# fp32-accurate column sums in two fp32r passes, one projection unit moved into the block inverse, and weight splits placed anew, in a two-layer hybrid decoder step

## The chip, the cores and the metric

The kernel runs on one core of one Trainium2 chip. The metric is the device time of one execution in microseconds (us). Before the change it is 3319.75 us, the median of 3 runs (3316.57 to 3322.81).

## What is computed

One inference step over 1056 tokens (a prompt of 1024 and 8 sample sequences of 4 tokens) through two decoder layers with width 1024, all in fp32:

```
layer 0: RMSNorm -> one input projection, whose columns feed
           A: dilated sliding-window softmax attention (3 groups of 4 heads, with caches for the samples)
           B: RWKV-7 time mixing, 12 heads of 64 (token shift, decay, delta-rule state, group norm)
         -> [A | B] -> output projection -> residual; RMSNorm -> squared-ReLU MLP (4096) -> residual
layer 1: RMSNorm -> HGRN2, 8 heads of 128 x 128 (forget gate, chunks of 64, output gate)
         -> output projection -> residual; RMSNorm -> squared-ReLU MLP -> residual; final RMSNorm
```

Besides the outputs of the last norm, the window rows of A, the shift rows and the states of B and HGRN2 are returned. In RWKV three sums over the 64 channels of a head and each token matter here: `ss`, the squared length of a key; `bo`, the bonus term r·k·r_k; and `mean` and `var` of the group norm.

## The kernel before, in words

**Tiling.** Activations lie feature-major: 128 partitions, 8 rows (KC) of features, 1056 tokens, worked in NT = 3 chunks of TC = 352 columns. Nearly all matmuls are fp32r, and fp32 accuracy comes from a split: each operand is kept as a high part (rounded to fp32r) and a low part (the rest), and a product is hi·hi + hi·lo + lo·hi. `Kernel.product` (L247) so issues 8 x 3 = 24 matmuls for a chunk of one output tile, called a unit here. `project(i, n, c)` in RWKV is the unit of pair i, tile n and chunk c, and `range(KC // 2)` makes half of one.

**Weights.** SP loads one weight tile of 512 KB at a time into a single buffer `w_raw` (`load_weight`, L209), once POOL has split the one before. POOL makes the high part (L232) and then the low part (L234) in `split_weight` (L223), into one of a few slots; PE waits for POOL's count of splits (`weight_ready`). The order of splits is that of the program, and each waits until PE has read the tile that was last in its slot. In HGRN the first head's four weights are loaded apart, split high by ACT and low by POOL (L4163).

**Stages.** Norm and start (0 to 60 us; `FirstNorm`: squares on ACT, sums over rows on DVE L335, normed rows on DVE L345 and their low parts on DVE L353), attention A (to 465 us), RWKV (465 to 1212 us), output projection 0, MLP 0 (1220 to 1954 us), HGRN (1965 to 2520 us), output projection 1, MLP 1, final norm. The order of the work of each engine is written out by hand; engines meet at named steps (`plan.at(...)`).

**RWKV.** `MixB` runs 6 pairs of heads, one loop turn each, plus a tail. In loop i PE works on pair i and, in between, makes the 9 projection units of pair i+1. The first part of a loop, here called the prelude, has the decay and gate projections (L2608, L2630), units of the next pair, and the sums over channels: `mean` and `var` of the pair before, `ss` and `bo` of this one, each 3 fp32 matmuls against `half_ones` (L2597). A matmul with fp32 operands is two instructions. In the prelude DVE has one long chain: token shifts (L3457 to L3463), the scan of the decays (L3319), and L3324 to L3362, with `rk` at L3359, `bT` at L3360 and `rT` at L3361. ACT does the exponentials, the norms and the evacuations of the units (L2529 to L2535). Then, twice, for blocks G = 0 and G = 1, come the transposes (`pe_turn`, L2725), scores (masked by DVE L3500), an inverse of 128 x 128 triangles by doubling, levels 2, 4, 8, 16 and 32 (`pe_T` L2809, `pe_YX` L2826 and L2829, evacuated by ACT and by DVE's predicated copies L3509), and `pe_solve` (L2850 to L2854). The sample tokens' small matmuls and DVE operations (L3562 to L3568, b_UV) stand in between. Output projection 0 (`EarlyProject`) reads RWKV's result back from DRAM as rows; POOL splits a row in L4398 and L4400, six of them in loop 4, and PE uses them from loop 5 on in place of the next pair's units. PSUM banks in RWKV: two for the units in turn, six for all else in turn (`Turns`; `B.emptied` waits for the last user).

**MLP.** Seven products over half tiles instead of eight, with combined weights (L1064, L1102); ACT evacuates the products (ff_b, L1196) in `keep_both` and stores the squares in `square_out` (L1206).

**HGRN.** Head h has four weight tiles (n = 0 to 3) in four slots, `slot(h, n) = (3, 2, 1, 0)[n]` in each head. The tail of head 7 is woven with output projection 1 (`SplitProject`), whose weights go to slots 0, 1, 2. DVE L4091 makes c_ks, which PE's L3849 reads.

## Time and profile before

| | |
|---|---|
| median of 3 runs | 3319.75 us |
| the profiled execution's own time | 3316.99 us |
| its span (first to last instruction) | 3315.2 us |
| mean granted TensorE clock | 0.983 |
| PE busy / weight load | 96% / 91% |
| DVE, ACT, POOL busy | 66%, 35%, 33% |
| DMA, mean | 97 GB/s |

The page's idle times are those of one engine before an instruction, with what ended them. PE's matmuls overlap in their records, so their starts tell more than their durations. Line numbers are those of the kernel before.

### The profile page before, as it was taken

The page shows a single profiled execution, that of the slowest core. Times are in us where ns is not written, and L with a number is a line of the kernel's source. Part 1 is how long each engine was busy: PE and PEld are TensorE (multiplying, and loading weights), DVE is VectorE, ACT ScalarE, POOL GpSimd, SP SyncE. Part 2 cuts the span into 40 slices and gives each one's busy share as a digit, 9 for nine tenths or more (in the row PEclk, how much of TensorE's full clock was granted, in tenths as well). Part 3 has the DMA queues.
Part 4 walks back from the last instruction along what each step waited for, and adds up shares of the span by engine and source line. Part 5 has one row for each costly group of instructions (what it writes and reads, how often), then busy time and mean ns, then how long its engine had stood idle before and what let it go on. Part 6 is the DMA issues. An engine that isn't in the chain of part 4 may idle for free. (4 is left out here: it accounts for less than half of the span.)

```text
span 3315.2 us, 74986 instructions
## 1 busy us (share of the span) xinstructions
PE 3178.5 (96%) x31728; PEld 3007.5 (91%) x31728; DVE 2171.6 (66%) x3016; ACT 1171.5 (35%) x2377; POOL 1089.3 (33%) x630
## 2 busy tenths in 40 slices
PE   7999889999999989999999999999998999999998
PEld 6999768888888879999999999999997999999998
DVE  5112774665666658666788884566546976668888
ACT  3344222332332434444433352221212444443334
POOL 3322110110114013444455533222202354445543
PEclk9999889999999999999999999999998999999999
DMA  5113540100101112444544411111113144455442
GB/s 167 65 59 103 184 134 9 33 30 9 37 30 53 59 35 74 147 142 141 199 143 143 143 59 58 60 66 60 59 53 117 49 146 143 143 192 169 143 143 92
DMA packets 151200, 322.71 MB, mean 97 GB/s; under 512 B 16904, under 2 KB 50356, under 8 KB 150744
## 3 DMA queue, kind: packets, MB, share of 16 engines
q1 hardware_dynamic: 106480, 242.53, 22.4%
q10 hardware_dynamic: 44392, 75.42, 6.7%
q8 instruction: 253, 4.15, 0.5%
q14 instruction: 75, 0.61, 0.1%
HBM read 227.12 MB, written 93.12 MB: 97 GB/s over the span
## 5 line engine op out<-in xcount | busy, mean ns | idle before, releaser
L247 PE MATMUL psum<-act_hi,w_hi 128*128 128x352 f32 x2088 | 704.7, 338 | 25.1 <-issue 7.3
L247 PE MATMUL psum<-act_hi,w_lo 128*128 128x352 f32 x2088 | 677.6, 325 | 0.0
L247 PE MATMUL psum<-act_lo,w_hi 128*128 128x352 f32 x2088 | 676.6, 324 | 0.0
L232 POOL TENSOR_TENSOR w_hi<-w_raw,derived 128x1024 fp32r<-128x1024 f32 x83 | 163.1, 1965 | 1421.8 <-PE psum L247 1342.9
L247 PEld LDWEIGHTS psum<-act_hi,w_hi 128*128 128x128 f32 x2088 | 397.4, 190 | 54.0 <-issue 23.1
L247 PEld LDWEIGHTS psum<-act_lo,w_hi 128*128 128x128 f32 x2088 | 398.6, 191 | 2.5 <-issue 0.2
L247 PEld LDWEIGHTS psum<-act_hi,w_lo 128*128 128x128 f32 x2088 | 397.8, 190 | 0.0
L1064 PE MATMUL psum<-ff_near,ff_w_hi 128*128 128x264 f32 x2048 | 379.5, 286 | 4.3 <-issue 1.5
L1064 PEld LDWEIGHTS psum<-ff_near,ff_w_hi 128*128 128x128 f32 x2048 | 317.5, 188 | 10.2 <-issue 9.6
L1064 PE MATMUL psum<-ff_far,ff_w_hi 128*128 128x264 f32 x1536 | 286.2, 287 | 8.9 <-ACT ff_b L1196 6.7
L1064 PE MATMUL psum<-ff_near,ff_w_lo 128*128 128x264 f32 x1024 | 291.1, 284 | 0.0
L1064 PEld LDWEIGHTS psum<-ff_far,ff_w_hi 128*128 128x128 f32 x1536 | 240.1, 190 | 10.3 <-issue 9.2
L1102 PE MATMUL psum<-ff_du_odd_lo,ff_dw_odd_hi 128*128 128x264 f32 x832 | 237.6, 286 | 0.0
L1102 PE MATMUL psum<-ff_du_odd_hi,ff_dw_odd_lo 128*128 128x264 f32 x832 | 237.4, 285 | 0.0
L1102 PE MATMUL psum<-ff_du_odd_hi,ff_dw_odd_hi 128*128 128x264 f32 x832 | 236.6, 284 | 0.0
L1471 DVE TENSOR_TENSOR x<-x,psum 128x528 f32<-128x528 f32 x272 | 183.0, 696 | 81.4 <-PE psum L1102 80.8
L1102 PE MATMUL psum<-ff_du_even_hi,ff_dw_even_lo 128*128 128x264 f32 x768 | 219.3, 286 | 0.0
L1064 PE MATMUL psum<-ff_far,ff_w_lo 128*128 128x264 f32 x768 | 219.1, 285 | 0.0
L1102 PE MATMUL psum<-ff_du_even_lo,ff_dw_even_hi 128*128 128x264 f32 x768 | 218.6, 285 | 0.0
L1102 PE MATMUL psum<-ff_du_even_hi,ff_dw_even_hi 128*128 128x264 f32 x768 | 217.9, 284 | 0.7 <-DVE ff_du_even_lo L1456 0.6
L234 POOL TENSOR_TENSOR w_lo<-w_raw,w_hi 128x1024 fp32r<-128x1024 f32 x83 | 214.6, 2586 | 6.5
L943 POOL TENSOR_TENSOR ff_w_lo<-ff_raw,ff_w_hi 128x512 fp32r<-128x512 f32 x94 | 149.5, 1605 | 153.8 <-ACT ff_w_hi L931 103.2
(565 smaller groups left out, 7370.7 us busy)
## 6 DMA issues: line engine op xcount, KB each, us to landing
ff_du_raw<-u SPq DMA_DIRECT2D x224, 264.0 KB, 2.8
w_raw<-weights SPq DMA_DIRECT2D x84, 512.0 KB, 3.3
u<-ff_stage SPq DMA_DIRECT2D x128, 264.0 KB, 2.3
ff_raw<-mlp SPq DMA_DIRECT2D x64, 512.0 KB, 3.9
u<-ff_side SPq DMA_DIRECT2D x96, 264.0 KB, 3.7
s_cache<-cache_a ACTq DMA_DIRECT2D x32, 512.0 KB, 7.1
ff_dt<-mlp SPq DMA_DIRECT2D x64, 256.0 KB, 4.5
ff_dt<-mlp SPq DMA_DIRECT2D x32, 512.0 KB, 7.2
```

The costliest lines, as they stand in the source:

```text
L232: pool.tensor_tensor(hi, raw, self.zeros, ALU.add).then_inc(s.sem, s.step())
L234: pool.tensor_tensor(lo, raw, hi.bitcast(F32), ALU.subtract).then_inc(s.sem, s.step())
L247: last = pe.matmul(out, w[:, k, :], h[:, k, cols], start=(start and k == ks[0] and m == 0), stop=(stop and k == ks[-1] and m == 2))
L943: engine.tensor_tensor(lo, self.weight(w, p), hi.bitcast(F32), ALU.subtract).then_inc(s.sem, s.step(label))
L1064: last = pe.matmul(out, weight[:, k], h[:, tp], start=(p in self.FRESH and k == 0 and t == 0), stop=(k == 3 and t == 2), skip_group_check= ...
L1102: last = pe.matmul(out, w[:, d], u[:, tp], start=(fresh and q == 0 and m == 0), stop=(q == self.WIDTH - 1 and m == 2), skip_group_check=True)
L1471: dve.tensor_tensor(dst, dst, src, op).then_inc(s.sem, s.step(f"dve.{n}.{label}{step}.{d}"))
```

## The change

It has seven parts. (1) Start: weights 1 and 2 are split by ACT (high) and DVE (low) in place of POOL, and the loads of the masks move on ACT's queue to behind `act_third`. (2) MLP: at w == 1 ACT evacuates (`keep_both`) ahead of `square_out` 11. (3) HGRN's first four weights get their low parts from DVE. (4) HGRN's slots rotate from head to head, and the early groups of output projection 1 move. (5) In RWKV POOL's splits of weights 0 and 1 of pairs 2 to 5, and of output projection 0, wait for quiet points of the loop two pairs before. (6) `var` (pairs 0 to 4), `ss` and `bo` are two fp32r passes, over a high part (ACT copy) and a low part (DVE subtract); `mean` and the last `var` stay fp32. Unit (i+1, 0, 2) and its evacuation go ahead of `var` and `ss`. (7) Unit (i+1, 2, 1) moves from behind `bo` into the first inverse, half before `pe_T` 32 and half before `pe_solve`, for i = 0 to 4. Memory is laid out anew for the added tiles.

```
--- before.py
+++ after.py
@@ -162,6 +162,7 @@
         self.half_ones = self.at("half_ones", [P, P], F32, o); o += 512
+        self.half_ones_r = self.at("half_ones_r", [P, P], F32R, o); o += 512
         self.masks = self.at("masks", [P, MASKS, P], U8, o); o += MASKS * P
@@ -232,6 +233,20 @@
         pool.tensor_tensor(lo, raw, hi.bitcast(F32), ALU.subtract).then_inc(s.sem, s.step())
+
+    def act_split(self, act, n):
+
+        s = self.plan.steps["act"]
+        act.wait_ge(self.sem("w_loaded"), (n + 1) * 16)
+        act.activation(self.slots[n][0].rearrange("p k c -> p (k c)"), self.w_raw[:, :], ACT.Copy)\
+            .then_inc(s.sem, s.step(f"act.weight{n}"))
+
+    def dve_split(self, dve, n):
+
+        s = self.plan.steps["dve"]
+        hi, lo = (w.rearrange("p k c -> p (k c)") for w in self.slots[n])
+        dve.wait_ge(*self.plan.at(f"act.weight{n}"))
+        dve.tensor_tensor(lo, self.w_raw[:, :], hi.bitcast(F32), ALU.subtract).then_inc(s.sem, s.step(f"dve.weight{n}"))
@@ -433,10 +448,13 @@
             self.act_square(act, t + 4)
+            if t == 5:
+                self.K.act_split(act, 1)
             self.act_square(act, t)
+        self.K.act_split(act, 2)
         self.act_root(act, 1)
@@ -470,10 +488,12 @@
         self.dve_part(dve, 0, 8)
+        self.K.dve_split(dve, 1)
         for t in range(8, 16):
     def dve_rest(self, dve):
+        self.K.dve_split(dve, 2)
         self.dve_part(dve, 8, 16)
@@ -1267,11 +1287,18 @@
                 self.weight_high(act, w + 1, p)
-            self.square_out(act, w, "11")
-            keep_both(w, 1)
-            for p in (6, 7):
-                self.weight_high(act, w + 1, p)
-            keep_both(w, 2)
+            if w == 1:
+                keep_both(w, 1)
+                self.square_out(act, w, "11")
+                keep_both(w, 2)
+                for p in (6, 7):
+                    self.weight_high(act, w + 1, p)
+            else:
+                self.square_out(act, w, "11")
+                keep_both(w, 1)
+                for p in (6, 7):
+                    self.weight_high(act, w + 1, p)
+                keep_both(w, 2)
             self.weight_high(act, w + 1, 5)
@@ -1541,6 +1568,8 @@
                     self.row_sum(dve, g, q)
+        if self.following is not None:
+            self.following.dve_weights(dve)
         for u in range(16):
@@ -1580,6 +1609,8 @@
         dve.wait_ge(K.sem("constants_loaded"), 6 * 16)
+        dve.tensor_tensor(K.half_ones_r[:, :], K.half_ones[:, :], K.derived[:, 1:2].broadcast_to([P, P]), ALU.add)\
+            .then_inc(K.plan.steps["dve"].sem, K.plan.steps["dve"].step())
         dve.tensor_copy(K.masks[:], K.masks_in[:]).then_inc(s.sem, s.step("dve.setup.masks"))
@@ -2077,7 +2108,12 @@
         K = self.K
+        s = K.plan.steps["pool"]
         for w in range(TILES_A):
+            if w in (1, 2):
+                pool.wait_ge(*K.plan.at(f"dve.weight{w}"))
+                pool.sem_inc(s.sem, s.step() + s.step())
+                continue
             if w >= W_SLOTS:
...
...
@@ -2597,6 +2642,15 @@
+        def split_sums(i, name, high, low):
+            for c in range(NT):
+                cols, out = slice(c * TC, (c + 1) * TC), ps[:, B.of(f"{i}.{name}{c}"), 0:TC]
+                pe.wait_ge(*B.emptied(f"{i}.{name}{c}"))
+                pe.wait_ge(*at(f"dve.B.{i}.{name}_low"))
+                pe.matmul(out, K.half_ones_r[:, :], high[:, cols], start=True, stop=False)
+                pe.matmul(out, K.half_ones_r[:, :], low[:, cols], start=False, stop=True)\
+                    .then_inc(s.sem, s.step(f"pe.B.{i}.{name}{c}"))
+
         for i in range(self.PAIRS + 1):
@@ -2615,12 +2669,13 @@
             unit(i + 1, 0, 1)
+            if not live:
+                sums(i - 1, "var", self.rs, f"act.B.{i - 1}.sq{{c}}")
+                break
+            unit(i + 1, 0, 2)
             if i:
-                sums(i - 1, "var", self.rs, f"act.B.{i - 1}.sq" + ("" if live else "{c}"))
-            if not live:
-                break
-            sums(i, "ss", self.e[4], f"act.B.{i}.kk2")
-            unit(i + 1, 0, 2)
+                split_sums(i - 1, "var", self.sum_high[0], self.rs_low)
+            split_sums(i, "ss", self.sum_high[1], self.e4_low)
             unit(i + 1, 1, 0)
@@ -2633,10 +2688,7 @@
             unit(i + 1, 2, 0)
-            sums(i, "bo", raw[1], f"dve.B.{i}.rk")
-            if i + 1 < self.PAIRS:
-                unit(i + 1, 2, 1)
-
+            split_sums(i, "bo", self.sum_high[0], self.raw_low[i % 2])
             self.pe_turn(pe, i, 0)
@@ -2657,9 +2709,13 @@
             self.pe_YX(pe, i, 0, 16)
+            if i + 1 < self.PAIRS:
+                begin(i + 1, 2, 1)
             self.pe_T(pe, i, 0, 32)
             self.pe_YX(pe, i, 0, 32)
+            if i + 1 < self.PAIRS:
+                end(i + 1, 2, 1)
             self.pe_solve(pe, i, 0)
@@ -3073,6 +3129,9 @@
                 act.activation(rs[:], before[2][:, 0:T], ACT.Square).then_inc(s.sem, s.step(f"act.B.{i - 1}.sq"))
+                act.wait_ge(*at(f"act.B.{i - 1}.sq"))
+                act.wait_ge(*at(f"pe.B.{i - 1}.GWa1e1"))
+                act.activation(self.sum_high[0][:, :], rs[:], ACT.Copy).then_inc(s.sem, s.step(f"act.B.{i - 1}.var_high"))
             evacuate(i + 1, 0, 0)
@@ -3080,6 +3139,8 @@
                     .then_inc(s.sem, s.step(f"act.B.{i}.kk2"))
+                act.wait_ge(*at(f"act.B.{i}.kk2"))
+                act.activation(self.sum_high[1][:, :], self.e[4][:], ACT.Copy).then_inc(s.sem, s.step(f"act.B.{i}.ss_high"))
             evacuate(i + 1, 0, 1)
@@ -3088,6 +3149,7 @@
                     .then_inc(s.sem, s.step(f"act.B.{i}.scale"))
+            evacuate(i + 1, 0, 2)
             if i:
@@ -3102,7 +3164,6 @@
                     .then_inc(s.sem, s.step(f"act.B.{i}.norm"))
-            evacuate(i + 1, 0, 2)
             if live:
@@ -3125,9 +3186,12 @@
             evacuate(i + 1, 1, 1)
+            act.wait_ge(*at(f"dve.B.{i}.rk"))
+            act.activation(self.sum_high[0][:, :], raw[1][:, 0:T], ACT.Copy).then_inc(s.sem, s.step(f"act.B.{i}.bo_high"))
             evacuate(i + 1, 1, 2)
             evacuate(i + 1, 2, 0)
-            evacuate(i + 1, 2, 1)
+            if i + 1 == self.PAIRS:
+                evacuate(i + 1, 2, 1)
@@ -3152,6 +3216,8 @@
                 .then_inc(s.sem, s.step(f"act.B.{i}.sGW"))
+            if i + 1 < self.PAIRS:
+                evacuate(i + 1, 2, 1)
             self.act_solve(act, i, 0)
@@ -3309,10 +3375,17 @@
                         .then_inc(s.sem, s.step(f"dve.B.{i - 1}.mean{c}"))
+            def low_part(owner, name, dst, src, high):
+                dve.wait_ge(*at(f"act.B.{owner}.{name}_high"))
+                dve.tensor_tensor(dst[:, :], src, high[:, :].bitcast(F32), ALU.subtract)\
+                    .then_inc(s.sem, s.step(f"dve.B.{owner}.{name}_low"))
+
             if live:
                 self.shifted(dve, i, 1)
+                if i:
+                    low_part(i - 1, "var", self.rs_low, self.rs[:], self.sum_high[0])
                 dve.wait_ge(*at(f"act.B.{i}.w2"))
@@ -3320,6 +3393,7 @@
                 done(dve.tensor_copy(self.mid[:, 0:NB], tiles[:, :, P // 2 - 1]), "mid")
+                low_part(i, "ss", self.e4_low, e4, self.sum_high[1])
                 dve.wait_ge(*at(L + "mid"))
@@ -3358,6 +3432,7 @@
             done(dve.tensor_tensor(r0, r0, e3, ALU.mult), "bT")
+            low_part(i, "bo", self.raw_low[i % 2], r1, self.sum_high[0])
             done(dve.tensor_tensor(r, r, e4, ALU.mult), "rT")
@@ -3575,7 +3650,13 @@
                     pool.wait_ge(*K.plan.at(before[n]))
+                if i >= 2 and n < 2:
+                    pool.wait_ge(*K.plan.at(self.quiet(i - 2, n)))
                 K.split_weight(pool, self.w0 + 3 * i + n, n)
+
+    def quiet(self, i, n):
+
+        return f"dve.B.{i}." + ("YX32_0w0", "S3")[n]
@@ -3756,8 +3837,15 @@
+    ORDERS = ((3, 2, 1, 0), (2, 3, 1, 0), (2, 1, 3, 0), (1, 2, 3, 0), (1, 2, 0, 3), (1, 0, 2, 3), (0, 1, 2, 3), (0, 1, 2, 3))
+
     def slot(self, h, n):
-        return (3, 2, 1, 0)[n]
+
+        return self.ORDERS[h][n]
+
+    def slot_freed(self, h, slot):
+
+        return f"pe.C.{h}.in{self.ORDERS[h].index(slot)}.{NT - 1}"
@@ -3776,6 +3864,14 @@
+    def dve_weights(self, dve):
+
+        s = self.K.plan.steps["dve"]
+        for n in range(4):
+            hi, lo = (flat(t) for t in self.K.slots[self.slot(0, n)])
+            dve.wait_ge(*self.K.plan.at(f"act.C.weight{n}"))
+            dve.tensor_tensor(lo, self.first_raw[n][:, :], hi.bitcast(F32), ALU.subtract).then_inc(s.sem, s.step(f"dve.C.weight{n}"))
+
     def out_rows(self, h, out):
@@ -3797,9 +3893,9 @@
             if h >= self.HEADS:
-                if 3 <= m < 6:
+                if m in (2, 3, 5):
                     for j in range(2):
-                        out.early_group(pe, j, m - 3, j, self.unit_before(h, j))
+                        out.early_group(pe, j, (2, 3, 5).index(m), j, self.unit_before(h, j))
                 elif 6 <= m < 10:
@@ -4158,12 +4254,11 @@
         for n in range(4):
-            hi, lo = (flat(t) for t in K.slots[self.slot(0, n)])
-            pool.wait_ge(*K.plan.at(f"act.C.weight{n}"))
-            pool.tensor_tensor(lo, self.first_raw[n][:, :], hi.bitcast(F32), ALU.subtract).then_inc(s.sem, s.step() + s.step())
+            pool.wait_ge(*K.plan.at(f"dve.C.weight{n}"))
+            pool.sem_inc(s.sem, s.step() + s.step())
         for h in range(1, self.HEADS):
             for n in range(4):
-                pool.wait_ge(*K.plan.at(f"pe.C.{h - 1}.in{n}.{NT - 1}"))
+                pool.wait_ge(*K.plan.at(self.slot_freed(h - 1, self.slot(h, n))))
                 K.split_weight(pool, self.w0 + 4 * h + n, self.slot(h, n))
@@ -4531,11 +4626,11 @@
             rwkv.pool(pool, [f"pe.low.in{n}.{NT - 1}" for n in range(3)])
-            out0.pool(pool, [f"pe.B.5.in{j}.{NT - 1}" for j in range(3)])
+            out0.pool(pool, [rwkv.quiet(rwkv.PAIRS - 2, 0), rwkv.quiet(rwkv.PAIRS - 2, 1), f"pe.B.5.in2.{NT - 1}"])
             K.plan.steps["split"].begin(pool)
             hgrn.pool(pool)
-            out1.pool(pool, [f"pe.C.{KC - 1}.in{n}.{NT - 1}" for n in (3, 2, 1)])
+            out1.pool(pool, [hgrn.slot_freed(KC - 1, slot) for slot in range(3)])
             mlp1.pool(pool)
@@ -4544,10 +4639,10 @@
             norm_mix0.act_first(act)
-            setup.act_masks(act, K)
             norm_mix0.act_second(act)
             norm_mix0.act_third(act)
+            setup.act_masks(act, K)
             attention.bias_spread(act)
```

## Rows read from the trace of the kernel before

**Rows 1.** The page, busy us, share of the span, instructions of each engine.

```profile
PE 3178.5 (96%) x31728; PEld 3007.5 (91%) x31728; DVE 2171.6 (66%) x3016; ACT 1171.5 (35%) x2377; POOL 1089.3 (33%) x630
```

**Rows 2.** PE in pair 1: start us, us, engine, line, operation, tiles, form.

```profile
603.28 1.94 PE L2597 MATMUL psum<-b_rs,half_ones 128*128 128x352 f32 x6
605.05 1.94 PE L2597 MATMUL psum<-b_e,half_ones 128*128 128x352 f32 x6
606.56 0.59 PE L247 MATMUL psum<-act_hi,w_hi 128*128 128x352 f32 x1
606.99 0.33 PE L247 MATMUL psum<-act_lo,w_hi 128*128 128x352 f32 x1
607.15 0.32 PE L247 MATMUL psum<-act_hi,w_lo 128*128 128x352 f32 x1
```

**Rows 3.** PE's waits: what it waited for, us in total, times, longest us.

```profile
PE psum L2850 <- DVE b_YX L3509: 9.5, 8, 1.3
PE psum L1064 <- ACT ff_b L1196: 6.7, 2, 3.4
PE psum L3849 <- DVE c_ks L4091: 6.4, 4, 4.5
PE psum L2809 <- DVE b_YX L3509: 5.5, 6, 0.9
PE psum L247 <- ACT b_raw L2535: 3.0, 1, 3.0
```

**Rows 4.** Timeline of DVE: start, pair 0 (two rows), loop 4.

```profile
21.87 2.66 DVE L353 TENSOR_TENSOR act_lo<-nm_h,act_hi 128x352 fp32r<-128x352 f32 x1
...
482.91 3.02 DVE L3460 SCALAR_TENSOR_TENSOR b_x<-b_x,vec,b_raw 128x1024 f32<-128x1024 f32 x1
...
499.15 1.25 DVE L3360 TENSOR_TENSOR b_raw<-b_raw,b_e 128x1056 f32<-128x1056 f32 x1
...
1049.16 2.79 DVE L3568 TENSOR_TENSOR b_UV<-b_UV,seq_mask 32x512 f32<-32x512 f32 x1
```

**Rows 5.** Timeline of PE in pair 1's first turn and first inverse.

```profile
634.43 0.60 PE L2725 MATMUL psum<-ident,b_e 128*128 128x128 f32 x4
...
656.17 1.15 PE L2809 MATMUL psum<-b_YX,b_L 64*64 64x64 f32 x32 [0.92 <-DVE b_YX L3509]
...
660.65 0.24 PE L2850 MATMUL psum<-b_YX,b_LZ 64*64 64x64 f32 x1 [1.13 <-DVE b_YX L3509]
```

**Rows 6.** Timeline of DVE in pair 1's prelude.

```profile
611.13 2.79 DVE L3341 SCALAR_TENSOR_TENSOR b_raw<-b_raw,vec,b_rs 128x1056 f32<-128x1056 f32 x1
613.96 3.32 DVE L3344 SCALAR_TENSOR_TENSOR b_raw<-b_raw,vec,b_raw 128x1056 f32<-128x1056 f32 x1
...
625.75 2.95 DVE L3360 TENSOR_TENSOR b_raw<-b_raw,b_e 128x1056 f32<-128x1056 f32 x1
628.62 3.41 DVE L3361 TENSOR_TENSOR b_x<-b_x,b_e 128x1056 f32<-128x1056 f32 x1
```

**Rows 7.** Timeline of POOL: pair 1's prelude, and loop 4.

```profile
612.89 3.28 POOL L234 TENSOR_TENSOR w_lo<-w_raw,w_hi 128x1024 fp32r<-128x1024 f32 x1
...
1042.23 1.95 POOL L4398 TENSOR_TENSOR act_hi<-out_raw,derived 128x1056 fp32r<-128x1056 f32 x1 [41.80 <-DMA out_raw<-mix]
```

**Rows 8.** Timeline of PE: start, loop 4, MLP, the MLP's end, HGRN's tail.

```profile
24.59 0.43 PE L247 MATMUL psum<-act_hi,w_hi 128*128 128x352 f32 x1 [3.47 <-DVE act_lo L353]
...
1052.84 0.34 PE L2826 MATMUL psum<-b_T,b_YX 64*64 64x64 f32 x1 [2.08 <-DVE b_UV L3562]
...
1325.53 0.78 PE L1064 MATMUL psum<-ff_far,ff_w_hi 128*128 128x264 f32 x2 [3.36 <-ACT ff_b L1196]
...
1943.94 0.56 PE L1102 MATMUL psum<-ff_du_last_hi,ff_dw_last_hi 128*128 128x264 f32 x1 [2.17 <-DVE ff_du_last_lo L1456]
...
2507.27 0.63 PE L247 MATMUL psum<-act_hi,w_hi 128*128 128x352 f32 x1 [7.35 <-issue]
```

**Rows 9.** Windows of HGRN's tail (us, busy of PE, PEld, DVE, ACT, POOL, PEclk, DMA).

```profile
2500.00:2505.00 5.00, 0.00 (x0) 0.00 (x0) 4.87 (x8) 0.00 (x0) 2.96 (x2) 0.50 1.03 419
```

More of the change, by code:

```diff
@@ L2419, in __init__ @@
         self.e = [take(f"e{n}", [P, T]) for n in range(5)]
+        self.L = take("L", [P, 2, 4, 64])
+        high_at = a
         self.YX = take("YX", [P, 2, 2, 4, 64])
-        self.L, self.T1, self.LZ = (take(n, [P, 2, 4, 64]) for n in ("L", "T1", "LZ"))
+        self.T1, self.LZ = (take(n, [P, 2, 4, 64]) for n in ("T1", "LZ"))
+        self.sYX = take("sYX", [NS, 2, 2, NS])
+        self.sum_high = [K.at(f"b_sum_high{n}", [P, T], F32R, high_at + n * WIDE) for n in range(2)]
+        assert high_at + 2 * WIDE <= a
         self.KA, self.RB, self.RK = (take(n, [P, 2, 4, P]) for n in ("KA", "RB", "RK"))
+        rs_at = a
         self.rs = K.at("b_rs", [P, T], F32, a)
@@ L2428, in __init__ @@
         self.S = take("S", [P, NB + 1, 64])
-        self.sYX = take("sYX", [NS, 2, 2, NS])
         self.sA = take("sA", [NS, 2, P])
@@ L2446, in __init__ @@
         self.reset = take("reset", [P, T], BF16)
+        raw0_at = a
         self.raw = [[take(f"raw0{n}", [P, RAW]) for n in range(3)], raw1]
+        self.rs_low = K.at("b_rs_low", [P, T], F32R, rs_at)
+        self.e4_low = K.at("b_e4_low", [P, T], F32R, e_at + 4 * WIDE)
+        self.raw_low = [K.at(f"b_raw_low{n}", [P, T], F32R, at + 4 * RAW) for n, at in enumerate((raw0_at, X_AT - 3 * 4 * RAW))]
         self.sL, self.sT1 = (take(n, [NS, 2, NS]) for n in ("sL", "sT1"))
```

## The prediction

> **What bounds the kernel now.** First the page's busy shares [rows 1]: PE is busy 3178.5 us, 96% of the span, the next engine 66%. So the end moves only by what PE issues less, by what PE no longer waits for, or by a clock regained. PE's ends are modelled, therefore I read starts: an fp32r matmul of 352 columns starts 0.16 us after the one before it (the last two lines of [rows 2]), so one projection unit (24 matmuls) is 3.8 us. Then the list of PE's waits [rows 3]: no wait is large, but several small ones stand just where the diff edits: b_YX in the RWKV inverses (9.5 + 5.5), ff_b in the MLPs (6.7), c_ks in HGRN (6.4), b_raw L2535 (3.0). Last the timelines around them.
>
> **The sum, part by part.** It is made against the profiled execution's own 3316.99 us; the median of the runs shown is 2.8 us higher, which I add at the end.
>
> **Column sums in two fp32r passes.** The three fp32 matmuls of a group run from 603.28 to 605.05, 1.77 us [rows 2]. After the change a group is six fp32r matmuls, 6 x 0.16 = 0.96. That is 0.81 less, for 5 var, 6 ss and 6 bo groups: **13.8 us**. The first fp32r matmul after fp32 costs 0.27 more than its pitch (606.56 to 606.99 [rows 2]); such turns go after ss and bo and come twice in the inverse (next part): nought.
> The Trainium skill (FP8 and Floating Point Precision, TensorE Precision Notes) says that true fp32 takes four passes through the array; by that a group would be 12 x 0.16 = 1.92 and the gain 17 x 0.96 = 16.3 us. The row's 1.77 decides.
> What it adds: 17 ACT copies and 17 DVE subtracts of 1056 columns. DVE gets 1.25 us each (the uncontended L3360 of pair 0 [rows 4]), ACT about as much at 1.1. ACT has room; the DVE part is priced below, since the RWKV prelude is where DVE matters.
>
> **The moved unit.** In each pair PE idles before pe_T 32 and before pe_solve: 0.92 and 1.13 us in pair 1 [rows 5]; with the 0.2 us or so that a modelled end hides, 1.1 and 1.3. The first inverses of the other pairs repeat it, and the two sums for b_YX in [rows 3] are these and their siblings in the second inverses, which stay. A half unit is 12 x 0.16 = 1.9 us, longer than either gap, so it fills both: 3.8 issued, 2.4 of it in idle time, and 3.8 gone from the prelude. Five pairs (0 to 4): **12 us**. Its evacuation goes behind sGW on ACT, just before act_solve; I cost it at nothing, since the next unit in that bank is one of the next prelude. If it delayed GW by its 0.47 us, that would take 2.4 us off over the five.
>
> **The prelude's DVE chain.** From 611.1 to 632.0 DVE runs without a break [rows 6], and the first turn starts at 634.43 [rows 5]. Two POOL splits lie beside it (the second half of the first: 3.28 us [rows 7]), and four operations take 2.79, 3.32, 2.95 and 3.41 us instead of 1.25 to 1.3: 7.4 us. The quiet waits take these splits off the stretch: weight 0 goes behind YX32, weight 1 behind S3, where DVE mostly reads PSUM; the weights are read a loop later. What is queued behind these waits on POOL is only the next weights' splits, and behind them on SP the next weight's load, which has the rest of the loop. Against the gain stand 3 new subtracts, 3.7 us, and one wait: L3344 needs ACT's norm, which without the stretched L3341 comes about 1 us late. So rT (L3361) ends 7.4 - 3.7 - 1.0 = 2.7 us earlier, near 629.3. PE comes earlier by the unit and three sum groups, 3.8 + 2.4 = 6.2: at 628.2. It would wait some 1.1 us, first at the bo sums (rk, ACT's copy, the subtract), then at the turn. With a handoff I take -1.3 us for each of pairs 1 to 5, **-6.5 us**; between 0 and -3 per pair. In loop 0 DVE idles ahead of bo, and nothing is lost.
> The change also puts unit (i+1,0,2) and its evacuation ahead of the norm: the 3.0 us wait for L2535 [rows 3], in which ACT stood behind a contended L3460 of 3.02 us [rows 4], goes, and 0.5 of startup with it: **3.5 us**.
>
> **out0's rows.** In loop 4 POOL splits six of out0's rows from 1042.23 on [rows 7], and beside them L3568 takes 2.79 us [rows 4] and PE waits 2.08 for b_UV [rows 8]. After the change these rows run behind S3, past the sample chain: 2.7 us gained. But they then end some 17 us later, 3 to 5 us before loop 5 first reads them, and POOL meets the next prelude. I take **0**, between +3 and -8.
>
> **Start.** POOL's split of weight 1 stretches L353 to 2.66 us where 0.52 is usual [rows 4]; PE waits 3.47 us at 24.59 [rows 8]. The second split does the same to the sums of squares. On ACT and DVE the splits stand in order with the sums, so none is stretched, but each takes 1.1 and 1.2 us of its engine, and the mask DMAs move on ACT to behind act_third, where three evacuations queue behind them. I take **4 us** (1 to 6).
>
> **MLP.** At w == 1 ff_b is evacuated behind square_out 11, which waits for DVE; PE waits 3.36 us [rows 8]. With keep_both ahead of it the wait goes, in both MLPs (6.7 for the two [rows 3]): **6.5 us** (4 to 7). The later store of the square delays nothing that PE reads soon.
>
> **Into HGRN.** POOL's four lows (L4163) run beside the last unit's lows on DVE, and PE waits 2.17 us at 1943.94 [rows 8] and 0.67 before it. On DVE the four take 4 x 1.2 us ahead of the last adds. **2 us** (0 to 3).
>
> **HGRN's tail.** PE waits 4.5 us for c_ks ([rows 3], longest) and 7.35 us for out1's weight 1 [rows 8]; PEclk falls to 0.50 [rows 9], the level of 1.2 GHz, after stretches in which PE stood. With the rotating orders slots 0 to 2 come free in head 7 in the order in which out1 wants them, so weights 0 and 1 can be split before 2490. What is then late next are early_group's rows, loaded in the same time, and c_ks. **8.5 us** (4 to 12): 7.4 of wait and about 4 of half clock, less 3 for the rows. In heads 1 to 6 each weight comes at most a unit later than before, with 25 us in hand: nothing.
>
> Sum: 13.8 + 12 - 6.5 + 3.5 + 0 + 4 + 6.5 + 2 + 8.5 = 43.8. 3317.0 - 43.8 = 3273.2; with 2.8 for the median 3276.
>
> **The rivals.**
> 1. **The low parts become the prelude's bound.** For: DVE's chain is already without a break, and PE arrives 6.2 us earlier. Against: 7.4 us of contention go. At -3.8 instead of -1.3 in five pairs 12.5 us more: 3288.
> 2. **The rows are late in loop 5.** For: 3 to 5 us of slack, and the prelude's two-input operations would be stretched again, each by 2 us. Against: only their last one or two lie there. 8 us: 3284. The Trainium skill (SBUF — State Buffer, Who interferes with whom) says that a DVE instruction with two SBUF inputs and a GpSimd instruction that reads SBUF exclude each other for the whole instruction. L3360 lost 1.7 us and L3344 2.0 beside splits of 1.9 to 3.28 us a half, part of them only; held to the letter the rule would make this rival 12 us, 3288.
> 3. **More than forecast.** The tail gives its 12, the start its 6, and the preludes wait half as long: 3.5 + 2 + 3.3 = 8.8: 3267.
> 4. **Slower.** One mechanism, in the preludes of pairs 1 to 5: copy, handoff and subtract stand in series on the one chain (3 x (1.1 + 1.25) = 7.1 us, and ACT reaches each copy an evacuation of 0.47 late, 1.4), while the splits still fall into the chain. The moved unit then covers nothing and its 3.8 us come back as a wait: 12.3 us a pair, 61.5 in five, in place of 6.5: 3319.75 - 50.3 + 61.5 = 3331. It ends slower from 10 us a pair on. Against it: ACT idles 1 to 3 us at the places where the copies go, and the quiet points lie in another half of the loop.
> That the start and the HGRN entry do nothing is possible: 3282.
>
> **How the numbers follow.** Forecast 0.48, rival 1 0.17, rival 2 0.10, rival 3 0.10, rival 4 0.04; start and entry without effect 0.06; several losses together that end within 0.2% 0.05. All best ends together are 60 us (3259), all worst 13 (3307). For 8 in 10 I leave out the outer ends: 3262 to 3298. A measurement tells about 0.2% (6.6 us) from no change: faster 0.91, same 0.05, slower 0.04.
>
> **What would show it.** In the profile after: fp32 sums left for mean and the last var alone, the new sums' six starts within 1 us; half units where rows 5 had idle; L3341 to L3361 at 1.3 us; a wait of 1 to 2 us at bo or the turn; no ff_b among the waits; out1's splits before 2490 and PEclk 1.00 in the tail. It is wrong if the bo sums or the turn wait over 3 us per pair, if out0's early groups wait in loop 5, or if RWKV as a whole gives less than 15 us (forecast 22.8).

## The result, and the profile after

The changed kernel takes 3280.94 us, the median of 4 runs (3280.22 to 3288.66), against 3318.16 us before (4 runs, 3314.06 to 3322.81): the ratio is 0.9893, 95% interval 0.9872 to 0.9913, so 37 us less. The forecast was 43.8 us less. The profiled execution has a span of 3279.1 us against 3315.2, 36.1 less.

From the page of the changed kernel, the line that answers to [rows 1], and the granted clock in 40 slices:

```profile
PE 3159.3 (96%) x31728; PEld 2993.9 (91%) x31728; DVE 2153.2 (66%) x3040; ACT 1188.3 (36%) x2396; POOL 1058.7 (32%) x622
...
PEclk9999889999999999999999999999999999999999
```

PE's busy time fell by 19 us; the other 17 of the 36 are idle time that went. The clock line is that of the kernel before but for one slice. The list of PE's waits in the changed kernel, for [rows 3]:

```profile
PE psum L262 <- DMA act_lo<-c_lo: 7.1, 1, 7.1
...
PE psum L413 <- DVE nm_acc L350: 4.4, 1, 4.4
...
PE psum L3945 <- DVE c_ks L4187: 3.9, 3, 2.8
PE psum L2906 <- DVE b_YX L3584: 3.8, 3, 1.3
PE psum L1084 <- ACT ff_a L1216: 3.6, 5, 1.1
...
PE psum L2650 <- DVE b_raw_low L3380: 2.6, 1, 2.6
...
PE psum L1084 <- DVE ff_r L1443: 2.1, 2, 1.7
...
PE psum L2865 <- DVE b_YX L3584: 0.9, 1, 0.9
```

The waits for b_YX fell from 9.5 and 5.5 us to 3.8 and 0.9, those for ff_b and b_raw L2535 are gone. New or grown are a DMA (7.1), nm_acc (4.4; before it was 3.4 in two waits, 2.35 at the start and 1.03 at the entry to HGRN, and the 4.4 all stand at that entry), ff_a (3.6 for 1.3), ff_r and b_raw_low. So several waits were replaced, not removed.

To see where the time went I laid the starts of the same matmuls in both traces side by side. It is one trace of each kernel, so a stage's shift also holds what the granted clock did there in that one execution. The shift (start after minus start before, us) at the stage borders, next to the forecast:

| stage | shift in it | forecast |
|---|---|---|
| start, to 60 us | -5.5 | -4 |
| attention, to RWKV | -0.4 | 0 |
| RWKV, loop 0 | -6.4 | |
| loops 1 to 4 | -21.6 | |
| loop 5 | +5.5 | |
| RWKV together | -22.5 | -22.8 |
| MLP 0 | -1.9 | -3.2 |
| into HGRN | -1.4 | -2 |
| heads and tail of HGRN | -2.9 | -8.5 |
| MLP 1 and the rest | -1.7 | -3.2 |

The new sums in pair 1, answering to [rows 2], and the first turn, answering to 634.43 in [rows 5]:

```profile
594.88 0.32 PE L2650 MATMUL psum<-b_sum_high,half_ones_r 128*128 128x352 f32 x1
595.04 0.32 PE L2651 MATMUL psum<-b_rs_low,half_ones_r 128*128 128x352 f32 x1
...
596.66 0.32 PE L2651 MATMUL psum<-b_e_low,half_ones_r 128*128 128x352 f32 x1
...
614.96 0.35 PE L2650 MATMUL psum<-b_sum_high,half_ones_r 128*128 128x352 f32 x1
...
615.78 0.33 PE L2651 MATMUL psum<-b_raw_low,half_ones_r 128*128 128x352 f32 x1
615.95 0.60 PE L2781 MATMUL psum<-ident,b_e 128*128 128x128 f32 x4
```

Twelve matmuls from 594.88 to 596.82 are two groups, 0.97 us each where 1.77 stood. The bo group starts without a wait, and so does the turn. The chain of DVE that feeds them, for [rows 6]:

```profile
601.13 1.31 DVE L3415 SCALAR_TENSOR_TENSOR b_raw<-b_raw,vec,b_rs 128x1056 f32<-128x1056 f32 x1
602.47 1.32 DVE L3418 SCALAR_TENSOR_TENSOR b_raw<-b_raw,vec,b_raw 128x1056 f32<-128x1056 f32 x1
...
612.26 1.25 DVE L3434 TENSOR_TENSOR b_raw<-b_raw,b_e 128x1056 f32<-128x1056 f32 x1
613.50 1.26 DVE L3380 TENSOR_TENSOR b_raw_low<-b_raw,b_sum_high 128x1056 fp32r<-128x1056 f32 x1
614.67 1.25 DVE L3436 TENSOR_TENSOR b_x<-b_x,b_e 128x1056 f32<-128x1056 f32 x1
```

The four operations that POOL had stretched and the new subtract (L3380) take 1.25 to 1.32 us each. L3418 starts with the end of L3415, so the 1.0 us wait for the norm that I had counted isn't there. The subtract ends at 614.76 and PE reads it at 614.96, so that handoff has no margin. rT (L3436, to 615.92) has one: the turn at 615.95 transposes other tiles, and the first matmuls that wait for rT come 3.4 us later:

```profile
619.35 1.16 PE L2839 MATMUL psum<-b_e,b_e 64*128 64x128 f32 x16
```

The same stretch in pair 5:

```profile
1056.29 2.22 PE L2662 MATMUL psum<-b_low,b_low_w 64*128 64x352 f32 x12
...
1072.31 0.40 PE L2650 MATMUL psum<-b_sum_high,half_ones_r 128*128 128x352 f32 x1 [0.96 <-DVE b_e_low L3380]
...
1093.23 0.40 PE L2650 MATMUL psum<-b_sum_high,half_ones_r 128*128 128x352 f32 x1 [2.58 <-DVE b_raw_low L3380]
...
1094.27 0.60 PE L2781 MATMUL psum<-ident,b_e 128*128 128x128 f32 x4
```

Here PE waits 0.96 and 2.58 us for low parts, and 1.0 us twice more in between. From the pair's first matmul to its turn it is 38.0 us; before it was 1123.64 - 1090.07 = 33.6:

```profile
1090.07 2.22 PE L2608 MATMUL psum<-b_low,b_low_w 64*128 64x352 f32 x12
...
1121.86 1.94 PE L2597 MATMUL psum<-b_raw,half_ones 128*128 128x352 f32 x6
1123.64 0.60 PE L2725 MATMUL psum<-ident,b_e 128*128 128x128 f32 x4
```

### The profile page after: what moved, and what is told of

Read it like the earlier page. It is cut to its first block and busy times, and to the rows that moved or that the text cites. A ratio compares the mean times of both kernels' runs of the same rounds, so it can differ in the third digit from the quotient of the medians.

```text
span 3279.1 us, 75033 instructions
## 1 busy us (share of the span) xinstructions
PE 3159.3 (96%) x31728; PEld 2993.9 (91%) x31728; DVE 2153.2 (66%) x3040; ACT 1188.3 (36%) x2396; POOL 1058.7 (32%) x622
## 5 line engine op out<-in xcount | busy, mean ns | idle before, releaser
L262 PE MATMUL psum<-act_hi,w_hi 128*128 128x352 f32 x2088 | 701.8, 336 | 22.8 <-DMA act_lo<-c_lo 7.1
L235 POOL TENSOR_TENSOR w_lo<-w_raw,w_hi 128x1024 fp32r<-128x1024 f32 x81 | 201.0, 2482 | 6.4
```

What stands on the lines that cost most here:

```text
L235: pool.tensor_tensor(lo, raw, hi.bitcast(F32), ALU.subtract).then_inc(s.sem, s.step())
L262: last = pe.matmul(out, w[:, k, :], h[:, k, cols], start=(start and k == ks[0] and m == 0), stop=(stop and k == ks[-1] and m == 2))
```

## The experiments

Each is the changed kernel with one edit, unless it says otherwise. In the code `...` stands for lines left out. Times of four runs differ by up to 10 us in these kernels, so beside the median I give the shift of the same matmuls against the changed kernel's trace, taken across the stage of the edit alone.

How far each can be trusted: the changed kernel was timed only in its own session. The kernel before, timed again beside the experiments, had medians of 3313.6 to 3316.3 us, not 3318.16, so a difference of medians against 3280.94 can be off by some 4 us. The ratio to the kernel before of the same session lies with its whole interval outside the changed kernel's (0.9893, 0.9872 to 0.9913) in three experiments only: the quiet waits taken away, the quiet waits alone, and the three edits together (0.9853, 0.9836 to 0.9869). The sums, the unit and the MLP's order come close to it (0.9919 to 0.9927, their intervals just overlap). The sizes of the smaller edits rest on one trace each, and the clock disturbs these too. Loop 0 is the same code in the changed kernel and in "The loads of groups 1 and 2 later", and there the granted clock stayed at 1.00 where the changed kernel's fell to half (both shown below, at the unit); the loop was 3.8 us shorter. So a stage's shift of less than about 4 us counts only where the waits in the trace explain it.

### The quiet waits taken away

```
-                if i >= 2 and n < 2:
-                    pool.wait_ge(*K.plan.at(self.quiet(i - 2, n)))
...
-            out0.pool(pool, [rwkv.quiet(rwkv.PAIRS - 2, 0), rwkv.quiet(rwkv.PAIRS - 2, 1), f"pe.B.5.in2.{NT - 1}"])
+            out0.pool(pool, [f"pe.B.5.in{j}.{NT - 1}" for j in range(3)])
```

> The changed kernel without the quiet waits: POOL splits the weights in the preludes again. Theory A (the quiet waits make the room in which the fp32r sums and the moved unit pay): in pairs 1 to 4 four DVE operations are stretched by 7 us in all, and since PE now reaches the bo sums without a margin it waits there or at the turn, 4 to 6 us a pair; with loop 0 (2 to 4) and loop 4's sample chain (3) 20 to 30 us slower than the changed kernel: 3301 to 3311. Rival B (the stretch stays hidden, the splits only move): under 8 us slower, 3281 to 3289.

Measured: 3329.86 us (10 runs), 1.0042 of the kernel before (1.0029 to 1.0054), slower than before. Against the changed kernel RWKV is 47 us longer by the trace: 7 in loop 0, 11, 8 and 8 in pairs 1 to 3, 14 in pair 4. PE's waits, then DVE and POOL in pair 1:

```profile
PE psum L2650 <- DVE b_raw_low L3380: 20.4, 6, 4.8
PE psum L262 <- ACT b_raw L2574: 12.0, 5, 3.2
```

```profile
600.66 1.86 DVE L3402 TENSOR_TENSOR b_scale<-b_e,b_mid 128x8 f32<-128x8 f32 x1
...
603.62 2.36 DVE L3528 COPY b_raw<-shift 128x8 f32<-128x8 f32 x1
...
621.19 2.95 DVE L3434 TENSOR_TENSOR b_raw<-b_raw,b_e 128x1056 f32<-128x1056 f32 x1
624.07 3.40 DVE L3380 TENSOR_TENSOR b_raw_low<-b_raw,b_sum_high 128x1056 fp32r<-128x1056 f32 x1
```

```profile
620.63 2.39 POOL L233 TENSOR_TENSOR w_hi<-w_raw,derived 128x1024 fp32r<-128x1024 f32 x1 [14.68 <-PE psum L262]
623.10 3.24 POOL L235 TENSOR_TENSOR w_lo<-w_raw,w_hi 128x1024 fp32r<-128x1024 f32 x1
```

Both bounds of the expectation were too low. The splits follow PE's reads, PE now reads earlier, and the second split falls just on bT and the new subtract: 2.95 and 3.40 us, with PE waiting behind them. DVE loses 3.8 us by it, no more than it lost before, when the split fell on bT and rT (2.95 and 3.41, [rows 6]). New is that PE has nothing left to do meanwhile.

The two engines took turns, operation by operation. The shortest high and low halves of a split in the kernel before take 1.89 and 2.35 us, the two DVE operations without POOL beside them 1.25 and 1.26. End to end that is 6.75 us, and here the four run from 620.63 to 627.47, 6.84 us. The high half waits for the operation before bT, bT for the high half, the low half for bT, and the subtract for the low half. The recorded 5.6 us of the split thus hold 1.4 us of POOL's own waiting. The rule of the Trainium skill that stood in rival 2 (SBUF — State Buffer, Who interferes with whom), by which the two exclude each other for a whole instruction, agrees with these times.

ACT is held too: in its program the evacuations stand behind the norm and the norm waits for DVE, and PE waits 12.0 us for b_raw.

### The quiet waits alone, on the kernel before

```
+                if i >= 2 and n < 2:
+                    pool.wait_ge(*K.plan.at(self.quiet(i - 2, n)))
```

(and the two labels for out0)

> The kernel before with the quiet waits alone. Theory A (before, PE had its unit (2, 1) as cover and did not wait for the stretched chain except at loop 0, loop 4): 4 to 8 us faster than before: 3311 to 3315. Rival B (the splits cost PE their 7 us in every pair): 25 us faster or more, 3293 and below.

Measured: 3310.23 us (10 runs), 0.9989 of before (0.9976 to 1.0002), 3.8 us less, which the interval does not tell from nothing. By the trace 4.3 us come in loop 0, 1.3 at out0's rows in loop 4, and the preludes of loops 1 to 4 together gain 0.8. Theory A holds. The same edit is worth 4 us alone, and 49 by the medians or 47 by the trace under the other parts.

### The sums in fp32 again

In effect (the kernel has it as a condition on the pair, which no pair meets here):

```
-                split_sums(i - 1, "var", self.sum_high[0], self.rs_low)
-            split_sums(i, "ss", self.sum_high[1], self.e4_low)
+                sums(i - 1, "var", self.rs, f"act.B.{i - 1}.sq")
+            sums(i, "ss", self.e[4], f"act.B.{i}.kk2")
...
-            split_sums(i, "bo", self.sum_high[0], self.raw_low[i % 2])
+            sums(i, "bo", raw[1], f"dve.B.{i}.rk")
```

(without the three copies and the three subtracts)

> The changed kernel with var, ss and bo in fp32 again, no copies and no subtracts, the order of the units as changed. Theory A (each group is worth 0.81 us, and pair 5's waits of 1.0, 1.0, 1.0 and 2.6 us come from the added chain): plus 13.8, minus 5 to 7 for pair 5: 7 to 9 us slower, 3288 to 3290. Rival B (the sums gave their full 13.8, pair 5's waits come from the order of the units alone): 13 to 14 slower, 3294 to 3295. Rival C (DVE's subtracts cost as much as PE gains): within 2 us of 3281.

Measured: 3289.68 us, 8.7 more than the changed kernel; by the trace 13.9 more up to loop 4 and 3.0 less in loop 5, 10.9 over RWKV (10.0 over the whole kernel). Theory A: the sums are worth their time in five pairs and cost in the sixth.

### Loop 5 as before

Var of pair 4, ss and bo of pair 5 in fp32, as above but for those alone, and in loop 5 the unit (with its evacuation) behind ss again:

```
-            unit(i + 1, 0, 2)
+            if i not in (5,):
+                unit(i + 1, 0, 2)
...
+            if i in (5,):
+                unit(i + 1, 0, 2)
             unit(i + 1, 1, 0)
```

> The changed kernel, but loop 5 as before: var of pair 4, ss and bo of pair 5 in fp32, without copies and subtracts, and unit (6, 0, 2) in its old place. Theory A (in pair 5 no POOL split stood in the prelude before, and PE had no unit to give away, so the added DVE and ACT work is paid in full; from the start of the pair to its first turn took 33.6 us before and 38.0 after): 4 us faster than the changed kernel, 3277, first turn 33.6 us behind the pair's start. Rival B (pair 5's loss comes from out0's rows and the load of x beside it, not from the sums): within 1.5 us of 3281, 37 to 38 us to the turn.

Measured: 3278.88 us, 2.1 less than the changed kernel in the medians; 4.4 less across loop 5 by the trace. Pair 5, first matmul, bo, turn:

```profile
1056.57 2.22 PE L2662 MATMUL psum<-b_low,b_low_w 64*128 64x352 f32 x12
...
1088.36 1.94 PE L2642 MATMUL psum<-b_raw,half_ones 128*128 128x352 f32 x6
1090.14 0.60 PE L2784 MATMUL psum<-ident,b_e 128*128 128x128 f32 x4
```

33.6 us again. Theory A, and the row loads beside it are cleared. With the sums alone undone loop 5 gained 3.0 (experiment before this one); the other 1.4 would be the unit's place.

### The unit back in the prelude

```
-                begin(i + 1, 2, 1)
...
-                end(i + 1, 2, 1)
...
+            if i + 1 < self.PAIRS:
+                unit(i + 1, 2, 1)
             self.pe_turn(pe, i, 0)
```

(and its evacuation likewise)

> The changed kernel with unit (i+1, 2, 1) whole behind the bo sums again. Theory A (both gaps of the first inverse are filled): 2.4 us a pair, 12 slower: 3293; in the profile the idle 0.9 and 1.1 us before pe_T 32 and pe_solve are back. Rival B (some of the gain went back as half clock or as a wait in the second inverse, as in pair 0, where 3.8 us more than in the trace of before went at the end of the sample chain): 6 to 9 slower, 3287 to 3290.

Measured: 3290.79 us, 9.9 more, and 10.6 in RWKV by the trace: between the two theories. The gaps are back in pair 1:

```profile
639.06 1.15 PE L2863 MATMUL psum<-b_YX,b_L 64*64 64x64 f32 x32 [0.92 <-DVE b_YX L3579]
...
644.11 0.34 PE L2904 MATMUL psum<-b_YX,b_LZ 64*64 64x64 f32 x1 [1.13 <-DVE b_YX L3579]
```

Loop by loop the difference runs from -2 to +8 us, not 2.4 each. Part of it is the granted clock. In loop 0 of the changed kernel it fell to half in the second inverse; the kernel before and, with the same code in loop 0, the kernel of the later loads kept 1.00 there (the changed kernel first, then these two):

```profile
536.00:540.00 4.00, 3.20 (x117) 3.03 (x117) 3.88 (x7) 0.97 (x3) 0.00 (x0) 0.90 0.02 4
540.00:544.00 4.00, 4.00 (x44) 2.39 (x38) 2.33 (x5) 0.00 (x0) 1.75 (x1) 0.50 0.02 4
```

```profile
552.00:556.00 4.00, 3.12 (x134) 2.95 (x131) 3.88 (x7) 0.97 (x3) 0.00 (x0) 1.00 0.01 4
556.00:560.00 4.00, 4.00 (x80) 3.02 (x76) 2.22 (x5) 0.36 (x1) 0.00 (x0) 1.00 0.02 4
```

```profile
538.00:542.00 4.00, 4.00 (x83) 3.02 (x77) 2.28 (x5) 0.30 (x1) 2.11 (x2) 1.00 0.01 4
```

The columns are the stretch and its length, PE, PEld, DVE, ACT and POOL busy, PEclk, DMA share and GB/s. PE's busy time ahead of it was alike (3.20 and 3.12 of 4 us). The half clock cost 3.8 us there, by the shift against either of the two. Some such stretches stand at one place in most of the traces and are missing in a few, and I can't assign them to an edit.

### The tail of HGRN: orders and groups as before

```
-    ORDERS = ((3, 2, 1, 0), (2, 3, 1, 0), ...
+    ORDERS = ((3, 2, 1, 0),) * 8
...
-                if m in (2, 3, 5):
+                if m in (3, 4, 5):
```

> The changed kernel with the slots in HGRN in one fixed order (3, 2, 1, 0) and the early groups at 3, 4 and 5 again. Theory A (the wait for weight 1 went, but another of 7.2 us, for the rows c_hi and c_lo, took its place, and of 8.5 us only 3.5 came): 3.5 us slower, 3284.5, with the 7.4 us wait behind a weight back. Rival B (the tail gave the forecast 8.5, and something else lost 5): 8 to 9 slower.

Measured: 3282.55 us, 1.6 more in the medians, which tells nothing (the ratio to the kernel before is 0.9886, 0.9859 to 0.9913); 3.5 more across the tail. The wait behind a weight is back at 7.27 us, and c_ks's longest is 4.48. Theory A, by the trace. In the changed kernel the tail has these two waits:

```profile
2469.44 0.66 PE L262 MATMUL psum<-act_hi,w_hi 128*128 128x352 f32 x1 [7.10 <-DMA act_lo<-c_lo]
...
2481.11 1.16 PE L3945 MATMUL psum<-c_qp,c_ks 128*64 128x64 f32 x20 [2.77 <-DVE c_ks L4187]
```

```profile
2464.00:2466.00 2.00, 0.00 (x0) 0.00 (x0) 2.00 (x3) 0.91 (x1) 0.00 (x0) 0.57 1.03 414
2466.00:2468.00 2.00, 0.00 (x0) 0.00 (x0) 1.97 (x4) 0.17 (x1) 0.00 (x0) 0.50 1.03 416
```

c_ks is waited for 2.77 us where it was 4.48, and in the place of the weight stands the rows' DMA, under way at over 410 GB/s. The clock falls as before.

### The early groups at 3, 4 and 5, with the rotating orders

```
-                if m in (2, 3, 5):
+                if m in (3, 4, 5):
```

> The changed kernel with the rotating orders, but early groups at 3, 4 and 5 as before. Theory A (group 0 waits for a DMA that lands at one fixed time, 9 us after its issue, wherever the group stands; one later place lets PE do a c_qp product inside that wait): 1 to 2 us faster, 3279 to 3280. Rival B (the c_qp product then waits 4.5 us for c_ks ahead of the group, and both waits add): 2 to 4 slower, 3283 to 3285.

Measured: 3277.63 us, 3.3 less in the medians and 4.0 less across the tail.

```profile
2471.65 1.98 PE L3945 MATMUL psum<-c_qp,c_ks 128*64 128x64 f32 x32 [4.00 <-DVE c_ks L4187]
...
2474.83 0.66 PE L262 MATMUL psum<-act_hi,w_hi 128*128 128x352 f32 x1 [0.95 <-DMA act_lo<-c_lo]
...
2485.03 0.43 PE L262 MATMUL psum<-act_hi,w_hi 128*128 128x352 f32 x1 [1.50 <-DMA act_lo<-c_lo]
```

The c_qp product waits 4.00 us for c_ks inside the time in which the DMA is under way, and then 0.95 and 1.50 are left for the rows: 6.5 us of waits for 9.9. Theory A, and more than it gave. The move of the groups to 2, 3 and 5 worked against the rotation: of its 7.5 us it gave 4 back.

### The loads of groups 1 and 2 later

```
-                for g in range(3):
-                    out.load(act, g)
+                out.load(act, 0)
...
+                if h == self.HEADS - 1 and m == 2:
+                    out.load(act, 1)
+                    out.load(act, 2)
```

> The changed kernel, in which ACT issues the loads of row groups 1 and 2 only behind its copy of row 6, some 4 to 6 us later. Theory A (6.3 MB leave together at about 410 GB/s and share it, so group 0's 2.1 MB land only after 9 us; alone they take 5.2): group 0's wait falls from 7.2 to 3 to 4 us, 1 to 3 us faster in all, 3278 to 3280, since groups 1 and 2 still land at 2475 to 2477. Rival B (the queue is served in order, so group 0 gains nothing and the others come later): 1 to 5 us slower.

Measured: 3276.93 us, 4.0 less in the medians, but 0.1 more across the tail: the medians' difference is from elsewhere. The wait for group 0 is 6.93 us where it was 7.10:

```profile
2465.49 0.66 PE L262 MATMUL psum<-act_hi,w_hi 128*128 128x352 f32 x1 [6.93 <-DMA act_lo<-c_lo]
```

Theory A falls. Group 0's second load was issued at 2456.58 and PE went on at 2465.49, 8.9 us; in the changed kernel it was issued at 2460.37 and PE went on at 2469.44, 9.1 us. The loads behind it came 4.7 us later in the one and within 3 us in the other, so they took nothing from group 0: ACT's queue moved its loads in order here. The later issue cost the other groups nothing either.

### The MLP's old order

```
-            if w == 1:
+            if w == 99:
                 keep_both(w, 1)
                 self.square_out(act, w, "11")
```

No w is 99, so every turn takes the other branch, with `square_out` ahead of `keep_both`.

> The changed kernel with the MLP's order of ACT as before (square_out 11 ahead of keep_both at w == 1). Theory A (of 3.4 us a wait for ff_b, 1.0 to 2.1 come back as waits for ff_a and ff_r of the next products, so 2.6 net in the first MLP and 1.5 in the second): 4 us slower, 3285, both waits of 3.4 us back. Rival B (the new waits have nothing to do with the order): 6.5 slower.

Measured: 3286.13 us, 5.2 more; by the trace 2.7 more across the edited products of MLP 0 and 1.4 across those of MLP 1. PE's waits with the old order:

```profile
PE psum L1084 <- ACT ff_b L1216: 6.7, 2, 3.4
...
PE psum L1084 <- ACT ff_a L1216: 1.3, 2, 0.7
```

The wait for ff_b is back, and that for ff_a is 1.3 where the changed kernel had 3.6, with ff_r's 2.1 not on the list. Theory A.

### HGRN's first low parts on POOL, and late on DVE

```
-            self.following.dve_weights(dve)
...
+            pool.tensor_tensor(lo, self.first_raw[n][:, :], hi.bitcast(F32), ALU.subtract).then_inc(s.sem, s.step() + s.step())
```

> The changed kernel with HGRN's first four low parts on POOL again. Theory A (PE's waits for ff_du_last_lo went, but DVE, which now has four more operations, became the bound: a wait of 4.4 us for nm_acc took their place; DVE's own balance is 7 us less stretch against 4.8 of work): 1.5 to 2 us slower, 3283, with the waits of 0.7 and 2.2 us back and nm_acc's near 1. Rival B (no effect, POOL or DVE): 3281.

Measured: 3283.25 us, 2.3 more, 1.1 across the stage. The 2.8 us for ff_du_last_lo are back, and nm_acc is at 1.7 instead of 4.4. The other way:

```
-            self.following.dve_weights(dve)
+            self.following.dve_weights(dve, (0,))
         for u in range(16):
             self.last_add(dve, u)
             self.after.dve_tail(dve, u)
+            if u == 8 and self.following is not None:
+                self.following.dve_weights(dve, (1, 2, 3))
```

> The changed kernel in which only weight 0's low part stands ahead of the last adds; 1, 2 and 3 come behind the ninth of them, where DVE is idle for 3.75 us. Theory A (DVE bounds the norm's sum there): the wait for nm_acc falls from 4.4 to about 1, 3 to 4 us faster, 3277 to 3278. Rival B (PE then waits for the act_lo rows, which come later by as much): within 1 us of 3281.

Measured: 3277.31 us, 3.6 less, and 5.0 less across the stage.

```profile
PE psum L413 <- DVE nm_acc L350: 1.0, 1, 1.0
```

Theory A both times: DVE was the new bound, and 3.4 us of the wait came from work that could stand later. The other 1.6 of the 5.0 is the clock: the changed kernel was granted 0.57 from 1921 to 1925, behind its longer wait, and this one 1.00 from 1920 to 1928. Whether the shorter wait kept the clock up isn't shown.

### Three edits together

Loop 5 as before, groups at 3, 4 and 5, the low parts behind the ninth add.

> The changed kernel with three edits together: loop 5 in fp32 and in the old order, the early groups at 3, 4 and 5, and the low parts of HGRN's weights 1 to 3 behind the ninth last add. Theory A (they stand in different stages and add): 4.4 + 4.0 + 3.5 = 12 us faster than the changed kernel, 3269. Rival B (half clock falls elsewhere and takes part of it): 3272 to 3276.

Measured: 3265.89 us (3263.59 to 3273.12), 0.9853 of before (0.9836 to 0.9869) and 15 less than the changed kernel. By the trace 4.4, 4.0 and 5.0 us in their stages, 13.3 together. It beats both kernels, and here the runs show it too: the ratio's interval lies below that of the changed kernel. The profiled execution as a whole is only 7.7 us shorter than the changed kernel's; it is the slowest of the four (3273.12). Rival B happened in it: the clock fell to half from 1023 to 1029 us and from 1139 to 1145, where the changed kernel's trace has 1.00:

```profile
1023.00:1029.00 6.00, 6.00 (x48) 4.11 (x48) 1.95 (x4) 0.00 (x0) 4.57 (x3) 0.50 0.01 3
```

## Why the prediction was right, and where it was not

- **Right in sign and range.** 3280.94 against 3276, in 3262 to 3298; 37 us of the 44 came. Some single terms were further off than the sum, so part of the agreement is luck. Of the signs that I named, the sums, the filled gaps, the 1.3 us operations and the missing ff_b came; PEclk 1.00 in the tail did not (0.50 from 2464 to 2474), and the wait at bo came in pair 5 alone.
- **Sums, 13.8.** The size of a group is right (0.97 us for 0.96, against the row's 1.77). The sum counted 17 groups; those of loop 5 brought no gain, since the chain there had no slack. What came is 8.7 by the medians, 10.9 across RWKV by the trace.
- **Unit, 12.** 9.9 with it undone. The mechanism holds (both gaps filled), the size was off, and half clock that fell in loop 0 and pair 1 of one trace and not of the other is part of that; how large a part stays open.
- **The prelude's -6.5.** The step that failed. I spread it as -1.3 over pairs 1 to 5. Pairs 1 to 4 show no wait for a low part: the 1.0 us wait for the norm did not come, and the turn, which I had waiting for rT, does not read it (its reader comes 3.4 us later). Pair 5 lost 6.8 alone, the 4.4 us by which its stretch grew and the 2.4 that three shorter groups should have taken off. I had seen that the quiet waits remove contention, and had not asked in which pair there was none: pair 5's L3341 to L3361 ran at 1.3 us before, so the subtracts are bare cost there, and PE, which before started the bo sums 31.8 us after the pair's first matmul, now waits until 36.9 for the last of them. The term came right by two errors that cancel, which is luck.
- **The quiet waits.** I costed the loss of cover at 7.4 us a pair. Taken away it is 47 us in all, 8 to 14 in each of pairs 1 to 4, as the splits are tied to PE's own progress and follow the chain. My rival 4 (12.3 us a pair, slower than before) is what then happens, at 10.2 on average. It needed exactly the condition that I gave it, that the splits still fall into the chain.
- **Loop 0, 3.5; rows, 0.** The waits of loop 0 gave 5.4 (4.1 for L2535, 1.3 at the first ss), and half clock in its second inverse took 3.8 away. Loop 4 gave 3.6 us more than its unit and sums. The rows account for 1.3 of it, which they gave alone; the rest may be the clock, granted 0.52 from 1052 to 1059 in the kernel before and 1.00 in this part of the changed kernel's trace. Rival 2 did not come: nothing waits for a row in loop 5. Its reading of L3360 and L3344, that they lost only part of a split, was wrong: they lost nearly what the split's halves take without DVE beside them, as the first experiment's times show.
- **Start, 4.** 5.5, in the range of 1 to 6. PE's waits of 3.47 and 2.35 us there fell to 0.2 and nothing, two new ones of 0.4 and 1.7 for the splits' count came, and the clock was at half three times between 18 and 39 us before and once after. It was not undone in an experiment, so which of its edits gave it, and how much is the clock, stays open.
- **MLP, 6.5.** 4.1. "The later store delays nothing that PE reads soon" was wrong: the next products wait 2.3 us more for ff_a and 2.1 for ff_r.
- **Into HGRN, 2.** 1.4, but the mechanism was only half seen: PE gained 6.3 us at the last units and gave 4.9 back, 3.4 of them to nm_acc (1.0 before, 4.4 now).
- **Tail, 8.5.** The term most wrong: 3.5. I named the rows as late next and took 3 us for them; it was 7.1, since group 0 was asked for earlier (at 2) and its two loads of 1056 KB come 9 us after their issue. The clock's loss, for which I had 4, stayed for the most part: half clock for 17 us before, for 13.5 after.

## What to carry to other kernels

When work leaves PE's stretch and other work is added to the engine that feeds it, ask for each turn of the loop apart what slack that engine has: the last turn differs. A contention that costs nothing today may be what bounds the kernel after the change, so edits that remove it are to be judged with the edits that need it, not alone (4 us alone, 47 together). After a wait is removed, lay the starts of both traces side by side: the wait that took its place stands a few us on, and was worth a second round of edits here (13 us).

## What was not expected

Half clock of TensorE (granted 0.50) came at 540 us in the changed kernel and at the same instructions neither in the kernel before nor in one with the same code there, with like busy time ahead of it, and cost 3.8 us. The DMA queue served one engine's loads in order: further loads of 1056 KB behind the first did not slow it (9.1 us with them right behind, 8.9 with them 4.7 us later). DVE and POOL kept each other out for whole instructions: two operations of 1.25 us each and a split of 4.2 us took 6.84 us together, and what DVE lost is the split's time without DVE beside it, not its recorded time.
